# A hybrid decoder step on one core: slots dealt over the partitions, expert outputs added by an accumulating scatter, and two smaller edits

## The reference

```python
x = layer_norm(ALPHA * x + mix, ln1_g[l], ln1_b[l])
ffn = hier_moe(x, w_group[l], b_group[l], w_router[l], b_router[l], w_gate[l], w_up[l], w_down[l])
x = layer_norm(ALPHA * x + ffn, ln2_g[l], ln2_b[l])

# in hier_moe: top-1 group, top-2 experts in it, softmax weights
h = jax.nn.silu(jnp.einsum('td,edf->tef', xf, w_gate)) * jnp.einsum('td,edf->tef', xf, w_up)
y = jnp.einsum('tef,te,efd->td', h, gate.astype(h.dtype), w_down)
```

## Time and profile before

| what | value |
|---|---|
| median of 3 runs | 1572.4 us (1566.12 to 1572.95) |
| profiled execution: its time | 1566.63 us |
| its span | 1564.6 us |
| mean granted TensorE clock | 0.962 of full |
| PE busy | 93% of the span |
| chain that ended last | PE 85%, DVE 10%, DMA 3% |
| blocks 2 to 16, one each | 35.15 us |
| last scatter landed to the end | 52.1 us |

### The profile page before, as it was taken

The page is one execution under the profiler, slowest core; times in us unless marked ns, Lnnn a source line. Parts: engine busy times, 40 slices in busy tenths (PEclk is TensorE's granted clock), DMA queues, the critical chain, the costliest instruction groups (busy, mean ns, idle before and its releaser), DMA issues.

```text
span 1564.6 us, 24064 instructions
## 1 busy us (share of the span) xinstructions
PE 1451.5 (93%) x9390; PEld 1292.0 (83%) x9390; DVE 1006.4 (64%) x1207; ACT 746.9 (48%) x862; POOL 165.3 (11%) x94
## 2 busy tenths in 40 slices
PE   7999999999999999999996889999999999999930
PEld 7998898889999999999995458888888888888720
DVE  4234525437777787623025558888888888888828
ACT  4224333334434433411110057888877777888712
POOL 0000000000000000233330001111121111111200
PEclk9999999999999999999997899999999999999965
DMA  8221321132213222523433499999999999999965
GB/s 285 85 82 55 108 85 59 54 109 91 83 55 110 84 81 70 184 88 124 153 109 135 163 376 357 403 385 383 376 374 374 395 404 392 395 389 380 362 222 215
DMA packets 90117, 337.76 MB, mean 216 GB/s; under 512 B 12264, under 2 KB 18944, under 8 KB 60588
## 3 DMA queue, kind: packets, MB, share of 16 engines
q1 hardware_dynamic: 85005, 319.66, 55.6%
q0 software_dynamic: 5040, 17.06, 2.9%
HBM read 320.96 MB, written 35.36 MB: 228 GB/s over the span
## 4 chain that ended last, share of the span: by engine, by line
PE 85%; DVE 10%; DMA 3%; issue 1%; SPq 0%; ACT 0%; ACTq 0%; DVEq 0%; POOL 0%; POOLq 0%
PE BANK L1542 13%; PE BANK L1543 12%; PE BANK L1544 12%; PE BANK L1875 7%; PE BANK L1877 7%; PE BANK L1876 7%; PE BANK L1914 4%; PE BANK L1912 4%; PE BANK L1913 4%; PE BANK L1859 2%; PE BANK L1594 2%; PE BANK L1617 2%; PE BANK L1673 2%; DVE LO L1016 1%; PE BANK L1888 1%
## 5 line engine op out<-in xcount | busy, mean ns | idle before, releaser
L1542 PE MATMUL BANK<-XH,HI 128*128 128x260 f32 x1786 | 519.0, 291 | 12.2 <-DVE XL L1013 8.9
L1543 PE MATMUL BANK<-XL,HI 128*128 128x260 f32 x1786 | 508.7, 285 | 0.0
L1544 PE MATMUL BANK<-XH,LO 128*128 128x260 f32 x1786 | 507.8, 284 | 0.0
L1435 DVE TENSOR_TENSOR LOB<-RAWB,HIB 128x2048 fp32r<-128x2048 f32 x196 | 448.9, 2293 | 84.7 <-ACT HIB L914 83.8
L914 ACT ACTIVATE HIB<-RAWB 128x2048 fp32r<-128x2048 f32 x196 | 376.3, 1920 | 116.8 <-PE BANK L1877 80.0
L1542 PEld LDWEIGHTS BANK<-XH,HI 128*128 128x128 f32 x1786 | 340.9, 191 | 28.6 <-issue 27.8
L1543 PEld LDWEIGHTS BANK<-XL,HI 128*128 128x128 f32 x1786 | 340.9, 191 | 0.0
L1544 PEld LDWEIGHTS BANK<-XH,LO 128*128 128x128 f32 x1786 | 340.8, 191 | 0.0
L1875 PE MATMUL BANK<-HIB,XGH 128*128 128x512 f32 x512 | 200.8, 392 | 0.8 <-DVE XGL L1445 0.8
L1877 PE MATMUL BANK<-LOB,XGH 128*128 128x512 f32 x512 | 199.5, 390 | 0.0
L1876 PE MATMUL BANK<-HIB,XGL 128*128 128x512 f32 x512 | 199.2, 389 | 0.0
(11 more groups left out here) (332 smaller groups left out, 1521.2 us busy)
## 6 DMA issues: line engine op xcount, KB each, us to landing
RAWB<-in_w_gate SPq DMA_DIRECT2D x68, 1024.0 KB, 9.3
RAWB<-in_w_up SPq DMA_DIRECT2D x68, 1024.0 KB, 9.4
RAWB<-in_w_down SPq DMA_DIRECT2D x68, 1024.0 KB, 10.3
RAW<-in_w_in SPq DMA_DIRECT2D x39, 1024.0 KB, 4.9
RAW<-in_w_out SPq DMA_DIRECT2D x16, 1024.0 KB, 5.1
Y<-in_xT SPq DMA_DIRECT2D x8, 520.0 KB, 9.0
RT<-in_xT SPq DMA_DIRECT2D x16, 260.0 KB, 5.2
x_rows<-R SPq DMA_DIRECT2D x5, 832.0 KB
```

The source lines that it names most:

```text
L1435: dve.tensor_tensor(LOB[:, s, :], RAWB[:, r, :], HIB[:, s, :].bitcast(F32), ALU.subtract).then_inc(b_lo[s], 1)
L1542: pe.matmul(bank, hw[:, c, :], h, start=(c == 0), stop=False)
L1543: pe.matmul(bank, hw[:, c, :], l, start=False, stop=False)
L1544: ins = pe.matmul(bank, lw[:, c, :], h, start=False, stop=(c == KC - 1))
```

## The change

It has five parts.

1. **Dealt slots.** `SLOT` holds `IOS` permuted: slots 0 to 7 lie on partitions 0, 4, ... 28, slots 8 to 15 on 64, 68, ... 92, slots 16 on start again one partition further, and slots 64 on again 32 further. The one-hots compare with `SLOT`.
2. **Accumulating scatter.** `y_rows` has 520 rows, one a token. SP fills it with x1 from `R` by five stores, between the weight loads of gate_up(1) and down(1); POOL waits for these (`s_y0`) after gather(1), and its scatters add to the rows. The target index is the token's.
3. **Tail.** No loads of x1, `YA` and `YB`: SP loads the four tiles of `y_rows` into `X2`, and the samples' rows behind the first. DVE's `added` is gone. ACT makes each tile's negative mean by one more pass (Copy with a scale and a running sum), ahead of the squares.
4. **Start.** Unit 0, and the first half of the chunks of unit 1's first half of tokens, are multiplied as plain float32 straight from `RAW` and `Y` (`unsplit`). The split of unit 0's weights is gone from ACT and DVE. SP's load of unit 2 waits for unit 0's products, that of unit 3 for unit 1's first half.
5. **x1 quarters.** They use banks 4 to 7 from the fifth on (`q_bank`), and a pair follows every weight chunk of `first_gate_up` instead of every second.

```diff
-    y_rows = nc.dram_tensor("y_rows", [2 * T, D], F32, kind="Internal").ap()
+    y_rows = nc.dram_tensor("y_rows", [T, D], F32, kind="Internal").ap()
...
+        def q_bank(q):
+            return 6 + q % 2 if q < EARLY_X1 else (6, 7, 4, 5)[q % 4]
...
                 if u == 2:
-                    sp.wait_ge(s_lo0, 4)
+                    sp.wait_ge(s_acc, 2)
                 elif u > 2:
                     sp.wait_ge(s_lo, u - 2)
+                if u == 3:
+                    sp.wait_ge(s_acc, 3)
...
             gate_up(1, 0)
+            for i in range(NT):
+                sp.dma_start(y_rows[i * TT:(i + 1) * TT, :], R[:, i, :]).then_inc(s_y0, 16)
             down(1, 8)
...
-            sp.wait_ge(s_x1w, 16 * (5 + NT))
-            for i in range(NF):
-                sp.dma_start(X2[:, i, :], x1_rows[128 * i:128 * i + 128, :]).then_inc(f_x, 16)
-            sp.dma_start(X8[:, :, :], x1_rows[SEQ:T, :].rearrange("(g r) (c n) -> (r c) g n", g=2, c=32)).then_inc(f_x, 16)
...
-            sp.dma_start(YA8[:, :, :], y_rows[0 * T + SEQ:0 * T + T, :].rearrange("(g r) (c n) -> (r c) g n", g=2, c=32)).then_inc(f_in8, 16)
-            sp.dma_start(YB8[:, :, :], y_rows[1 * T + SEQ:1 * T + T, :].rearrange("(g r) (c n) -> (r c) g n", g=2, c=32)).then_inc(f_in8, 16)
             for i in range(NF):
-                for c, dst in ((0, YA), (1, YB)):
-                    sp.dma_start(dst[:, i, :], y_rows[c * T + 128 * i:c * T + 128 * i + 128, :]).then_inc(f_in[i], 16)
+                sp.dma_start(X2[:, i, :], y_rows[128 * i:128 * i + 128, :]).then_inc(f_in[i], 16)
+                if i == 0:
+                    sp.dma_start(X8[:, :, :], y_rows[SEQ:T, :].rearrange("(g r) (c n) -> (r c) g n", g=2, c=32)).then_inc(f_in8, 16)
...
                     in_=YO[:, :], in_offset=None,
-                    bounds_check=last_row, oob_is_err=False).then_inc(b_yw, 16)
+                    bounds_check=last_token, oob_is_err=False, compute_op=ALU.add).then_inc(b_yw, 16)
...
             gather(1, b_xg)
+            pool.wait_ge(s_y0, 16 * NT)
             pool.memset(ROWS[:, :], 0.0).then_inc(s_ones, 1)
...
+            act.sem_inc(s_hi, 1)
             for g in range(8):
-                if g % 2 == 0:
-                    cols = slice(256 * g, 256 * g + 512)
-                    act.wait_ge(s_w0[g // 2], 16)
-                    act.activation(HI[:, 0, cols], RAW[:, 0, cols], ACT.Copy).then_inc(s_hi if g == 6 else s_hi0, 1)
                 act.wait_ge(s_x[g], 16)
...
+                act.wait_ge(f_in[i], 16)
+                act.activation(YB[:, i, :], X2[:, i, :], ACT.Copy, scale=-1.0 / D, accum_out=MV2[:, i, 0:1]).then_inc(f_mu, 1)
                 act.wait_ge(f_mu, i + 1)
...
+                    slots = IOS[:, :].rearrange("p (k r g e) -> p g k e r", k=2, r=4, g=2)
+                    places = SLOT[:, :].rearrange("p (g k e r) -> p g k e r", g=2, k=2, e=8)
+                    for g in range(2):
+                        for k in range(2):
+                            dve.tensor_copy(places[:, g, k, :, :], slots[:, g, k, :, :])
...
-            def added(i):
-                dve.wait_ge(f_in[i], 32)
-                done(tt(X2[:, i, :], X2[:, i, :], YA[:, i, :], ALU.add))
-                done(dve.scalar_tensor_tensor(X2[:, i, :], X2[:, i, :], 1.0, YB[:, i, :], ALU.mult, ALU.add, accum_out=MV2[:, i, 3:4]))
-                ts(MV2[:, i, 0:1], MV2[:, i, 3:4], -1.0 / D, None, ALU.mult).then_inc(f_mu, 1)
...
+            def unsplit(u, hf, c):
+                w = RAW[:, u % 2, :].rearrange("p (c n) -> p c n", c=KC)
+                ins = pe.matmul(acc(2 * u + hf), w[:, c, :], Y[:, c, hf * HALF:(hf + 1) * HALF], start=(c == 0), stop=(c == KC - 1))
+                if c == KC - 1:
+                    ins.then_inc(s_acc, 1)
...
-                if hf == 0 and kq == 0:
+                if m == 2 and kq == 0:
+                    pe.wait_ge(s_raw[1], 16)
+                    for c in range(8):
+                        unsplit(u, hf, c)
+                    return
...
-                        if c % 2 and q < 4 * NT:
+                        if q < 4 * NT:
                             shift_quarter(q)
                             shift_quarter(q + 1)
                             q += 2
```

More of the change, by code:

```diff
@@ L203, in build @@
     O_8 = O_PR + NF * D * 4
-    X8, YA8, YB8, Q8 = (sb(n, [128, 2, 64], F32, O_8 + 512 * k) for k, n in enumerate(("X8", "YA8", "YB8", "Q8")))
+    X8, Q8 = (sb(n, [128, 2, 64], F32, O_8 + 512 * k) for k, n in enumerate(("X8", "Q8")))
     LG8, LB8 = (sb(n, [128, 64], F32, O_8 + 2048 + 256 * k) for k, n in enumerate(("LG8", "LB8")))
@@ L347, in build @@
         s_passed = sem("waits_passed")
-        f_x = sem("x1_in")
+        s_y0 = sem("y_rows_set")
         f_in = [sem(f"y_in{i}") for i in range(NF)]
@@ L364, in build @@
         IOS = small("IOS", [TT, 128])
+        SLOT = small("SLOT", [TT, 128])
         THB = small("THB", [TT, MAXB + 2])
@@ L665, in _ @@
             pool.wait_ge(s_ones, 2)
-            last_token, last_row = pool.to_reg(T - 1), pool.to_reg(2 * T - 1)
+            last_token = pool.to_reg(T - 1)
             def gather(j, landed):
@@ L1007, in _ @@
             for g in range(8):
[L1008 to L1011, removed]
                 dve.wait_ge(s_xh, g + 1)
@@ L1393, in _ @@
                RS4[:, :, :].bitcast(F32).unsqueeze(1).to_broadcast([TT, 2, NT, 4]), ALU.mult)
-            tt(OH[:, :, :, :].rearrange("p c i n -> p (c i) n"), bc(IOS[:, :].unsqueeze(1), TT, 2 * NT, 128), bc(pos.unsqueeze(2), TT, 2 * NT, 128),
+            tt(OH[:, :, :, :].rearrange("p c i n -> p (c i) n"), bc(SLOT[:, :].unsqueeze(1), TT, 2 * NT, 128), bc(pos.unsqueeze(2), TT, 2 * NT, 128),
                ALU.is_equal).then_inc(r_tab, 1)
@@ L1399, in x1_quarter @@
                 dve.wait_ge(s_q, q + 1 if q < 2 else q + 5)
-                dve.scalar_tensor_tensor(R[:, i, c0:c0 + 512], R[:, i, c0:c0 + 512], MV[0:TT, i, 2:3], BANK[0:TT, 6 + q % 2, :], ALU.mult, ALU.add).then_inc(s_x1, 1)
+                dve.scalar_tensor_tensor(R[:, i, c0:c0 + 512], R[:, i, c0:c0 + 512], MV[0:TT, i, 2:3], BANK[0:TT, q_bank(q), :], ALU.mult, ALU.add).then_inc(s_x1, 1)
             def first_tokens(g):
@@ L1414, in _ @@
             ts(TIX[:, :], tab[:, 0, :], ROW_SKIP, LIM[:, 0:1], ALU.add, ALU.min)
-            ts(YIX[:, :], tab[:, 3, :], ROW_SKIP, None, ALU.add)
+            ts(YIX[:, :], tab[:, 0, :], ROW_SKIP, None, ALU.add)
             done(dve.tensor_copy(TABF[:, :], tab[:, 1, :]))
@@ L1485, in samples_sum @@
             def samples_sum():
-                dve.wait_ge(f_in8, 32)
-                done(tt(X8[:, :, :], X8[:, :, :], YA8[:, :, :], ALU.add))
-                done(tt(X8[:, :, :], X8[:, :, :], YB8[:, :, :], ALU.add))
+                dve.wait_ge(f_in8, 16)
                 dve.tensor_reduce(S8[:, 0:2], X8[:, :, :], AX.X, ALU.add).then_inc(f_s8, 1)
@@ L1548, in first_unit @@
             def first_unit():
-                hw = HI[:, 0, :].rearrange("p (c n) -> p c n", c=KC)
-                lw = LO[:, 0, :].rearrange("p (c n) -> p c n", c=KC)
                 for c in range(KC):
                     if c % 4 == 0:
-                        pe.wait_ge(s_hi0, c // 4 + 1) if c < 12 else pe.wait_ge(s_hi, 1)
-                        pe.wait_ge(s_lo0, c // 4 + 1)
+                        pe.wait_ge(s_w0[c // 4], 16)
                     if c % 2 == 0:
-                        pe.wait_ge(s_xl, c // 2 + 1)
+                        pe.wait_ge(s_x[c // 2], 16)
                     for hf in range(2):
-                        products(acc(hf), hw, lw, hf, c, s_acc)
+                        unsplit(0, hf, c)
+            def unsplit(u, hf, c):
[3 more added lines that the diff above has]
+                    ins.then_inc(s_acc, 1)
             def quarter(u, hf, kq):
                 m = 2 * u + hf
-                if hf == 0 and kq == 0:
+                if m == 2 and kq == 0:
[3 more added lines that the diff above has]
+                    return
+                if hf == 0 and kq == (1 if u == 1 else 0):
                     pe.wait_ge(s_hi, u + 1)
                     pe.wait_ge(s_lo, u)
+                if m == 2:
+                    pe.wait_ge(s_xl, 8)
                 if kq == 0 and m >= 3:
@@ L1805, in shift_quarter @@
                     pe.wait_ge(s_l5, 2)
-                if q >= 2:
-                    pe.wait_ge(s_x1, q - 1 if q - 1 <= EARLY_X1 else q + 3)
-                pe.matmul(BANK[0:TT, 6 + q % 2, :], L5[:, i * TT:i * TT + TT], GB5[:, c0:c0 + 512], start=True, stop=True).then_inc(s_q, 1)
+                if 2 <= q < EARLY_X1:
+                    pe.wait_ge(s_x1, q - 1)
+                elif q >= EARLY_X1 + 4:
+                    pe.wait_ge(s_x1, q + 1)
+                pe.matmul(BANK[0:TT, q_bank(q), :], L5[:, i * TT:i * TT + TT], GB5[:, c0:c0 + 512], start=True, stop=True).then_inc(s_q, 1)
             pe.wait_ge(r_hot, 1)
```

6 lines of the change are left out of this document (removed).

## The result

The changed kernel took 1555.8 us (median of 4 runs, 1555.5 to 1561.5) beside 1572.7 us of the kernel before in the same session: a ratio of 0.9902, 95% interval 0.9875 to 0.9929, so 1.0% faster. On a second chip the same pair gave 0.9903 (0.9873 to 0.9932), 1558.9 us against 1573.3. The profiled execution took 1555.7 us with a span of 1553.9, 10.7 us less than the span of before; the sum had said 8.0 less.

A forecast was written before the change was run, and what follows sets the result against it. PE was taken as the bound, with the DMA engines close behind. Start -0.7, x1 -3.6, stores +15.1, tail -18.8 and blocks 0 sum to -8.0 us; set on the median, 1564.4 us, range 1547 to 1581, likeliest case 1556 to 1573.

The forecast's parts named there:

- Tail: After the last scatter: DVE makes two passes of a tile instead of four, 4.8 us a tile; gain 18.8 us.
- The stores: Block 1 to 2: five y_rows stores delay gather 2, PE stalls 12.6 us, slow clock adds 2.5; loss 15.1 us.
- A store of 104 rows runs at 221 GB/s alone ... I take 3.9: Stores before block 2: each priced at 3.9 us for 0.85 MB, the five ending at 941.3.
- The bound of 3.1 us: Stores before block 2, low case: 3.1 us each if the next transfer fills spare engine time; with gather, loss 9 us.
- The down loads ... are hidden in that: Block 1's down loads, behind the stores, land by 945, hidden in PE's stall of 12.6 us.
- x1 and the first gather: Stage around x1: earlier quarter pairs bring the first gather 4.4 us sooner, shrinking PE's stall; gain 3.6 us.
- Start: First units: raw products end unit 1 at 35.5, but late constants delay unit 2's LO; net gain 0.7 us.
- Blocks and the accumulate: Blocks: PE-bound, so dealing gives 0 us; scatter's own price taken as 0, from -3 to +10.
- waits of ACT for weight tiles in the later blocks: Later blocks: a profile sign that would show the forecast wrong; 35.15 us a block was expected.
- The rival of the held engine: Every block scatter: each accumulated row holds its engine 1.7 us, blocks become DMA-bound; 1617 us, chance 0.10.
- the dip to 336 GB/s: Blocks before the change, gather and scatter moving: 336 GB/s instead of 420, taken to fit dense rows on half the engines.
- The median: Whole kernel: the summed change was set on the runs' median, 1572.4 us, 5.8 above the profiled execution; 1564.4 us.

The follow-up runs named there:

- e10: Changed kernel with the tail's means taken by a reduction on DVE instead of ACT's Copy pass; 1565.7 us, ratio 0.9953 to the kernel before.
- e9: Changed kernel without x1's stores: y_rows zeroed early, x1 loaded into X2 in the last block, tail loads accumulate; 1553.4 us, 0.9874 of before.
- e11: Changed kernel with five more stores of the same R tiles, onto p_rows, gather 2 waiting for all ten; 1573.3 us, ratio 0.9995 to before.
- e5: Kernel before with the dealing of slots alone, scatter and rows unchanged; 1570.0 us, ratio 0.9988.
- e1: Changed kernel with POOL waiting for the five stores ahead of each scatter instead of ahead of gather 2; 1556.8 us, ratio 0.9895 to before.
- e4: e1 with each of the five stores split into one of 96 rows and one of 8; 1556.5 us, ratio 0.9892 to before.
- e6: Kernel before with the new start alone, first unit as unsplit products on the raw tiles; 1571.4 us, ratio 0.9992.
- e2: Changed kernel with a plain scatter that writes instead of adding, sums left out; 1553.5 us, ratio 0.9886 to before.
- e3: Changed kernel with one-hots made from IOS again, so dense slots, accumulating scatter kept; 1589.7 us, ratio 1.0113 to before.
- e12: The changed kernel itself measured again, beside e13 on one chip; 1558.9 us, ratio 0.9903 to before.
- e13: The kernel of e9 measured again beside the changed kernel on one chip; 1553.0 us, ratio 0.9859 to before.
- e7: Kernel before with x1's quarters in pairs over four banks alone; 1569.9 us, ratio 0.9980.

## Why the prediction was right, and where it was off

**Tail: right.** Two of DVE's four passes gone, 18.8 us forecast and 19.4 measured; tiles of 4.72 us for 4.8. e10 puts one pass back and pays three tiles of it.

**The stores: the mechanism was right, the price too high.** The stall, who released it, POOL's wait on `y_rows` and the low clock behind it all came as forecast; e9 takes the stores away and the stall goes. The mis-sized term is "A store of 104 rows runs at 221 GB/s alone ... I take 3.9". In the mix it is 2.8 us (e11); the stores ended at 935.6 and not 941.3. The bound of 3.1 us was the nearer one, and it was the one that filled the spare time of a store with the next transfer. That was partly made up by the gather: 10.2 us and not the 8.0 that dealing was to give. Dealing gives none of it: the gathers of the blocks land after 9.0 us in before and in e5 alike, and after 9.2 to 10.0 beside added rows. So the stage cost 11.3 for 15.1. The forecast put the whole stall on the gather. e1 and e4 show that the down tiles, behind the same stores, are late too, 6.9 and 4.4 us: with one wait gone the other takes its place. "The down loads ... are hidden in that" was right, and only as long as the longer wait stood over them.

**x1 and the first gather: too much.** Forecast 3.6, measured 2.3. PE's wait for XG only shrank, from 4.42 to 2.10 us. The gather left 3.0 us sooner where the forecast, with the start, had 5.1. The rate was right: from 881.3 to 900.0 the queues moved 326 GB/s in 93% of the engines' time, so 350 when busy for the forecast's 347. The bytes were not: that is 6.1 MB for 5.5, since two more weight tiles, issued at 891.82 and 895.08, moved beside the last stores.

**Start: too little.** Forecast 0.7, and 2.1 us at unit 2. From the first constant's issue to the last one's were 4.9 us (22.89 to 27.80) and not 7.2, but `LO` began 4.8 us behind that and not 3.4; it ended at 34.9 and not 36.7, cost 0.7 and not 1.2 us, and the raw products ended unit 1 at 34.6 and not 35.5. Of the 2.1 us only 1.3 are left at the gather of p_rows, e6's trace keeps 0.8, and its time shows nothing. So the forecast's 0.7 is not refuted by more than one execution differs from the next.

**Blocks and the accumulate: the weighing was right, the margin thinner than told.** The forecast said that waits of ACT for weight tiles in the later blocks would show it wrong. They were there, 15.8 us of waits, but they moved only three blocks, by 2.6 us. The rival of the held engine took 1.7 us for each accumulated row and put the point of decision at 1.1; q0's time in e2 and in the changed kernel gives some 0.3 us more for a row (an estimate), about what 8 KB take once more at the forecast's 26 GB/s. So no row holds its engine for anything like that. That a block can be bound by its DMA engines all the same is what e3 shows: with the same bytes and dense rows the kernel is some 33 us slower than the changed one. The dealt one stays near the border, on its good side. That PE bounds the blocks of before was no reason to put dealing at 0 us for the changed kernel: it is what makes the rest possible, and by itself it is worth nothing (e5). What the scatter costs on its landing, 0 forecast, was -0.8 us: it was 8.4 to 9.0 us in the eight profiles with dealt and added rows, 7.4 and 8.7 with dealt and plain ones (e2, e5). The reading of the dip to 336 GB/s as a sign of dense rows was wrong for the most part, as e5 shows. The rule of the Trainium skill (DMA: Bandwidth & Descriptors, "Rules for kernel authors"), by which an accumulating DMA reads its destination and writes it later, agrees with q0's time, 11.4% for 7.9%, and with 219 GB/s for 424.

**The sum.** Its -8.0 for -10.7 is in part luck: the stage with the stores came out 3.8 us cheaper than forecast, the last block, the last landing and the tail 2.2 and the start 0.6, while x1's gain was 1.3 smaller and the late blocks, at 0 in the sum, took 2.6.

**The median.** Of the 8.6 us between forecast and result only 2.7 are in the sum. The other 5.9 come of setting the sum on the median of the runs, 5.8 us above the profiled execution: the changed kernel's profiled execution is at its own median. What such a slower execution of the kernel before may look like is seen in e6, which is before but for its start: 4.6 us more by the gather of p_rows, 2.4 us of late blocks, 19.06 us in place of 17.50 for the last step. The changed kernel shows the first of these too (e12, gather of p_rows at 867.6), and late blocks in both of its profiles (1.1 us in e12), so the second is already in its sum. Why its runs lie closer to its best profile than those of the kernel before was not tried; it stays open.

## What to carry to other kernels

Price a transfer by what it adds to the mix it runs in, not by its rate when it runs alone with one kind of neighbour; and when a wait is on two things that come late for one reason, moving one of them wins only the difference. An accumulate costs its DMA engine about the same bytes once more, so it fits where the fullest engine, not the mean one, has that much time left; spreading the rows may be worth nothing before (e5) and some 33 us after (e3). Initial values that are known late are dear at the busiest place of the kernel: set zeros while the queues are idle, and add the late part where they are idle again (e9 and e13, 1.3 and 1.4% below the kernel before).

## What the runs showed of the hardware that was not expected

Where the low clock falls decides several microseconds, and it is not tied to the edits. Windows of e7, PE's busy time, granted clock, DMA share, GB/s:

```profile
880.00:890.00 10.00, 10.00 (x14) 0.50 0.20 50
890.00:900.00 10.00, 10.00 (x14) 0.50 0.65 226
```

Here PE was busy throughout at half the clock, 14 instructions in 10 us for 24 or 25 in the changed kernel, after a stretch in which it was busy for 4.7 and 6.1 us of two times 10. In e9 it was busy for 4.6 and 6.0 of the same two, and the granted clock was 1.00 from 880 us on; what decides stays open. It cost 9 us between the gather of p_rows and gather 1 (48.2 us for 39 to 41). e1 and e13 had the same in their profiled executions, e4, e9 and e12 did not, and the other runs of e1 were 11 to 14 us faster than its profiled one. So a difference below 10 us between two single executions of this kernel says little; the intervals above, and stretches at the same clock, do.
